# Four buffers for the experts' down weights instead of two, two of them in the memory of the transposed activations

## The chip, the cores and the metric

The kernel runs on one core of one Trainium2 chip. The metric is the device time of one execution in microseconds (us), the median of several runs.

## The reference

The kernel computes a two-layer encoder trunk for 1024 tokens of width 1024, all in float32. Layer 0 mixes tokens with a gated short convolution, layer 1 with multi-head latent attention. After each mixer stands a mixture of experts (MoE) with 64 experts; each token picks one group of eight and two experts in it. Cut to what matters here:

```
h = rms_norm(x, ffn_norm_w[i])
x = x + hier_moe(h, ...)            # once after each of the two mixers

# inside hier_moe, for every expert e of 64, over the rows sent to it:
hid = silu(xblk @ w_gate[e]) * (xblk @ w_up[e])    # 1024 -> 384
y   = hid @ w_down[e]                              # 384 -> 1024
out[token] += gate * y
```

Each of the three matrices of an expert has 1024 x 384 float32 values. There are 2 x 64 experts, 2048 assignments of a token to an expert per layer, so 32 rows for an expert on average.

## The kernel before

There are four stages one after the other: convolution, MoE of layer 0, attention, MoE of layer 1. The change is in the two MoE stages (`moe_phase`). An expert is handled in a round of at most 64 rows (`RANKS`); the loop over experts is executed 64 times in each layer here. For each expert `g`:

- GpSimd (POOL) gathers the expert's rows from `h_rows` in DRAM by an indirect DMA into `gathered` and, later, scatters the result from `y` into `y_rows`. Both use POOL's own DMA queue (q0).
- TensorE (PE) runs, in this order in its instruction stream: `gate_and_up(g)` (16 matmuls, L1230), `turn_x(g+1)` (4 transposes, L1220), `down(g-1)` (6 matmuls, L1249), `turn_h(g)` (3 transposes, L1239). So the down product of an expert stands behind the gate and up products of the next one.
- VectorE (DVE) and ScalarE (ACT) copy, multiply and apply the activation between these.
- SyncE (SP) loads the weights on one hardware DMA queue (q1): the gate matrix, the up matrix and the down matrix, 1536 KB each.

The weights have two buffers each ("slots"), expert `g` using slot `g % 2`. SP's loop walks over the experts. For expert `g` it waits until gate and up of expert `g-2` have been multiplied, issues the gate and the up load, then waits until the down product of `g-2` is done, issues the down load, and goes on to `g+1`. All counters of TensorE's products start at `AHEAD` = 2, so a wait for `g + free(0)` = `g + 1` asks for the product of expert `g - 2`. The loads of experts 0 and 1 are issued already in the stage before (`sp_store_rows`). Nothing but these waits sets when a load is issued, and SP issues them strictly in the order in which they are written.

`hT` is a tile of 128 x 8 x 1024 float32, the transposed activations, which the mixers use and which the MoE stage uses only as scratch while it works out the routing. `rows` (128 x 4 x 1024 float32) holds normalised rows before they are stored.

Of the kernel before, what the change touches and what calls it, by code (L numbers as in the profile page):

```python
# [16 lines left out]
F32 = mybir.dt.float32  # L17
I32 = mybir.dt.int32
BF16 = mybir.dt.bfloat16
# [5 lines left out]
P = 128  # L25
D, S = 1024, 1024
KD = D // P
NT = S // P
EPS = 1e-6
BANK = 512  # L30
NE, NG, EG = 64, 8, 8
NL = NG + NE
FF = 384
KF = FF // P
# [9 lines left out]
PARTS = ((HIGH, HIGH), (HIGH, LOW), (LOW, HIGH))  # L44
LATENT_AT = 12 * D
AHEAD = 2


def wait(eng, sem, value):
# [25 lines left out]
class Core:  # L75


    def __init__(self, nc, ins, out, ctx):
        self.nc, self.ins, self.out = nc, ins, out

        def sb(name, shape, dt=F32):
            return ctx.enter_context(nc.sbuf_tensor(name, shape, dt))

        self.x = sb("x", [P, NT, D])
        self.hT_at = -(-nc.sbuf_base // 32) * 32
        self.hT = sb("hT", [P, KD, S])
        self.rows = sb("rows", [P, 4, D])
        self.turned = sb("turned", [P, 2, KD, P])
        self.logits = sb("logits", [P, NT, NL])
# [299 lines left out]
class ExpertWeights:  # L389


    def __init__(self, c, layer):
        self.sems = Sems(c.nc, f"weights{layer}")
        self.gate_up_loaded = [self.sems(f"gate_up_loaded{i}") for i in range(2)]
        self.down_loaded = [self.sems(f"down_loaded{i}") for i in range(2)]
        self.piece = c.carve()
        self.gate = self.piece(2, 2, 4 * FF)
        self.up = self.piece(2, 2, 4 * FF)
        self.down = self.piece(2, KF, D)
        self.gate_dram = c.ins["exp_w_gate"][layer].rearrange("e (h p j) f -> p e h (j f)", h=2, p=P)  # L400
        self.up_dram = c.ins["exp_w_up"][layer].rearrange("e (h p j) f -> p e h (j f)", h=2, p=P)
        self.down_dram = c.ins["exp_w_down"][layer].rearrange("e (j p) d -> p e j d", p=P)
# [5 lines left out]

    def load_down(self, sp, slot, e):
        src = self.down_dram[:, bass.ds(e, 1), :, :].rearrange("p a j d -> p (a j) d")  # L410
        sp.dma_start(self.down[:, slot, :, :], src).then_inc(self.down_loaded[slot], 16)  # L411


class OutProjection:
# [449 lines left out]
def moe_phase(c, layer, last, experts):  # L864
# [4 lines left out]
    nc, ins = c.nc, c.ins  # L869
# [11 lines left out]
    idx_f = piece(4, NE)  # L881
    tiny = piece(16, NT)

    piece = c.carve(c.hT[:, :, :].rearrange("p k s -> p (k s)"))
    onehot = c.typed(f"onehot{layer}", 0, [P, 2 * NT, P], BF16, c.hT_at)
    piece(NT * P)
    by_rank = piece(2 * NT * NE)
    by_pick = piece(2, NT, EG)
# [46 lines left out]
    def free(g):  # L935
        return g + 1
# [8 lines left out]
    with nc.Block() as block:  # L945

        @block.sync
        def _(sp):
            count = rounds(sp)
            with sp.Fori(1, count * (NE // 2)) as pair:  # L950
                g = pair * 2
                for slot in range(2):
                    e = (g + slot) % NE
                    sp.wait_ge(gate_up_products, g + slot + free(0))
                    experts.load_gate_up(sp, slot, e)
                    sp.wait_ge(y_products, g + slot + free(0))
                    experts.load_down(sp, slot, e)

            sp.wait_ge(y_stored, count * NE + AHEAD)
            for t in range(NT):  # L960
                if t >= Y_RING:
                    sp.wait_ge(x_added, t - Y_RING + 1)
                src = c.y_rows.rearrange("(k t p) d -> t p k d", k=2, p=P)[t]
                sp.dma_start(y_pair[:, t % Y_RING, :, :], src).then_inc(y_pair_loaded[t % Y_RING], 16)
            if not last:
                LatentPlaces(c).load(sp, c, latents_loaded)
            if last:
                for t in range(NT):
                    sp.wait_ge(x_added, t + 1)
                    sp.dma_start(c.out[0, t * P:(t + 1) * P, :], c.x[:, t, :]).then_inc(stored, 16)  # L970
                sp.wait_ge(stored, 16 * NT)
# [230 lines left out]
        def _(pe):  # L1202
# [37 lines left out]
                                         gate_up[:, slot, j * P:(j + 1) * P], c.ident[:, :])  # L1240
                last_.then_inc(h_turned, 1)

            def down(g, slot):
                pe.wait_ge(hidden_ready, g + done(0))
                pe.wait_ge(w_down_loaded[slot], g * 8 + (16 - 8 * slot))
                pe.wait_ge(y_copied, g + free(0))
                for j in range(KF):
                    for half in range(2):
                        last_ = pe.matmul(c.ps[half * RANKS:(half + 1) * RANKS, 6 + slot, :], hidden[:, slot, j, :],  # L1249
                                          w_down[:, slot, j, half * BANK:(half + 1) * BANK],  # L1250
                                          start=(j == 0), stop=(j == KF - 1))
                last_.then_inc(y_products, 1)

            with pe.Fori(0, count) as r:
# [5 lines left out]
                last_.then_inc(idx_products, 1)  # L1260
                g0 = r * NE

                turn_x(g0, 0)
                gate_and_up(g0, 0)
                turn_x(g0 + 1, 1)
                turn_h(g0, 0)
                with pe.Fori(0, NE // 2 - 1) as pair:
                    for n in (1, 2):
                        g, slot = g0 + pair * 2 + n, n % 2
                        gate_and_up(g, slot)  # L1270
                        turn_x(g + 1, 1 - slot)
                        down(g - 1, 1 - slot)
                        turn_h(g, slot)
                gate_and_up(g0 + NE - 1, 1)
                down(g0 + NE - 2, 0)
                turn_h(g0 + NE - 1, 1)
                down(g0 + NE - 1, 1)
            if norm:
                for t in range(NT):
                    norm.pe_turn(pe, t)  # L1280
# [606 lines left out]
```

## Time and profile before

| | us |
|---|---|
| median of 3 runs | 2976.38 |
| lowest and highest run | 2976.2, 2980.21 |
| span of the profiled execution, first to last instruction | 2971.0 |
| median less span | 5.38 |

The profile shows one execution. Its span leaves out what lies around the first and the last instruction; the median of the runs stands 5.38 us above it. TensorE is busy for 81% of the span, VectorE 26%, ScalarE 22%, GpSimd 17%; the hardware queue q1 moves 666.65 MB and q0 33.64 MB. A busy share is an average over four stages with different limits, and the two MoE stages, from about 450 to 1276 us and from 2108 to 2932 us, take 1650 us of the span together.

### The profile page before, as it was taken

What the parts mean: (1) busy time and instruction counts of PE and PEld (TensorE: products, weight loads), DVE (VectorE), ACT (ScalarE), POOL (GpSimd) and SP (SyncE); (2) the same over time, 40 slices, a digit from 0 to 9 for tenths busy, and PEclk for the clock granted to TensorE, in tenths of its full rate; (3) what the DMA queues carried; (4) which work ended last, traced back from release to release, by engine and by line L of the source; (5) the groups of instructions that cost most, each with busy time, mean ns of one, the idle gap of its engine ahead of it and who ended that gap; (6) DMA issues with size and microseconds to landing.
All of it is one profiled execution on the core that took longest, in us unless ns stands there. A gap on an engine that the chain in (4) does not pass through costs nothing. (4 is left out here: it accounts for less than half of the span.)

```text
span 2971.0 us, 35580 instructions
## 1 busy us (share of the span) xinstructions
PE 2421.0 (81%) x11822; PEld 1434.1 (48%) x11822; DVE 787.3 (26%) x2377; ACT 640.3 (22%) x1328; POOL 514.2 (17%) x775
## 2 busy tenths in 40 slices
PE   7999877778878777758699999989587788787773
PEld 5888663333333333335588888768233333333331
DVE  4222650000000000050666666526200000000003
ACT  3111211111001101131255555542001111001011
POOL 2121312111111111110111111021111111111110
PEclk9999988899898988969899999999789998989897
DMA  4112037999999999950000000101799999999997
GB/s 118 43 43 85 29 156 293 390 372 390 383 388 386 395 381 390 383 187 0 8 8 9 8 15 0 57 15 73 279 381 380 395 384 383 389 383 392 382 386 298
DMA packets 202294, 701.12 MB, mean 236 GB/s; under 512 B 36192, under 2 KB 65888, under 8 KB 202224
## 3 DMA queue, kind: packets, MB, share of 16 engines
q1 hardware_dynamic: 181744, 666.65, 56.7%
q0 software_dynamic: 20480, 33.64, 3.0%
q8 instruction: 31, 0.51, 0.1%
q14 instruction: 39, 0.32, 0.0%
HBM read 687.59 MB, written 46.14 MB: 247 GB/s over the span
## 5 line engine op out<-in xcount | busy, mean ns | idle before, releaser
L1230 PE MATMUL ps<-arena 128*64 128x384 f32 x4096 | 822.4, 563 | 326.3 <-DMA arena<-in_exp_w_up 323.9
L1230 PEld LDWEIGHTS ps<-arena 128*64 128x64 f32 x4096 | 327.2, 158 | 765.6 <-issue 714.5
L1133 DVE TENSOR_TENSOR arena<-ps,xw 128x512 f32<-128x512 f32 x128 | 88.5, 691 | 1122.2 <-PE ps L1220 1122.2
L1249 PE MATMUL ps<-arena 128*64 128x512 f32 x1536 | 357.7, 600 | 2.2 <-DVE arena L1142 2.2
L1040 ACT ACTIVATE arena<-ps 128x384 f32<-128x384 f32 x128 | 62.9, 491 | 1086.2 <-PE ps L1230 1086.2
L815 PE MATMUL ps<-hT_split,w_split 128*128 128x512 f32 x1152 | 264.5, 391 | 3.1 <-DVE hT_split L291 3.1
L815 PEld LDWEIGHTS ps<-hT_split,w_split 128*128 128x128 f32 x1152 | 217.0, 189 | 49.0 <-DVE hT_split L291 3.9
L996 POOL COPY col_idx<-scatter_idx 128x1 int32 (+1 forms) x128 | 23.4, 182 | 1104.1 <-ACT arena L1051 1104.1
L1249 PEld LDWEIGHTS ps<-arena 128*64 128x64 f32 x1536 | 99.3, 136 | 164.3 <-issue 149.3
L1051 ACT ACTIVATE arena<-ps 128x512 f32<-128x512 f32 x128 | 76.4, 597 | 372.4 <-PE ps L1249 372.4
L989 POOL DMA_INDIRECT arena<-h_rows,col_idx x128 | 134.5, 1051 | 115.3 <-POOL col_idx L986 108.3
L999 POOL DMA_INDIRECT y_rows<-arena,col_idx x128 | 131.4, 1027 | 113.2 <-POOL col_idx L996 113.2
L1142 DVE TENSOR_TENSOR arena<-arena,ps 128x192 f32<-128x192 f32 x128 | 45.3, 354 | 397.4 <-ACT arena L1046 397.4
L1797 PE MATMUL ps<-arena 128*128 128x256 f32 x512 | 117.7, 384 | 7.4 <-ACT arena L1519 7.4
L1220 PEld LDWEIGHTS ps<-ident,arena 128*128 128x128 f32 x512 | 71.8, 209 | 89.0 <-issue 89.0
L1771 PE MATMUL ps<-k_split,q_split 128*128 128x512 f32 x384 | 114.7, 407 | 0.0
L1797 PEld LDWEIGHTS ps<-arena 128*128 128x128 f32 x512 | 98.1, 192 | 22.3 <-issue 8.7
L1220 PE MATMUL ps<-ident,arena 128*128 128x128 f32 x512 | 96.5, 312 | 13.2 <-DMA arena<-h_rows,col_idx 13.2
L1447 POOL TENSOR_TENSOR turned<-turned,minus_half 128x2 f32<-128x2 f32 x64 | 44.1, 689 | 355.9 <-ACT rows L1500 310.1
L1505 ACT ACTIVATE rows<-ps,turned 128x1024 f32<-128x1024 f32 x64 | 71.4, 1115 | 138.6 <-DVE turned L1675 138.6
L1672 DVE TENSOR_REDUCE turned<-ps 128x1 f32<-128x1024 f32 x64 | 78.3, 1224 | 69.4 <-PE ps L1773 67.3
L1239 PEld LDWEIGHTS ps<-ident,arena 128*128 128x128 f32 x384 | 39.8, 140 | 105.1 <-issue 102.2
(201 smaller groups left out, 2783.2 us busy)
## 6 DMA issues: line engine op xcount, KB each, us to landing
arena<-in_exp_w_gate SPq DMA_DIRECT2D x128, 1536.0 KB, 11.2
arena<-in_exp_w_up SPq DMA_DIRECT2D x128, 1536.0 KB, 14.4
arena<-in_exp_w_down SPq DMA_DIRECT2D x128, 1536.0 KB, 8.3
arena<-y_rows SPq DMA_DIRECT2D x16, 1024.0 KB, 10.9
arena<-in_conv_w_in SPq DMA_DIRECT2D x24, 512.0 KB, 3.6
h_rows<-rows SPq DMA_DIRECT2D x16, 512.0 KB, 2.6
x<-in_x SPq DMA_DIRECT2D x8, 512.0 KB, 7.5
arena<-in_conv_w_out SPq DMA_DIRECT2D x2, 2048.0 KB, 9.9
```

What stands on the lines that cost most here:

```text
L815: last = pe.matmul(c.ps[:, 3 * h + j, :], w_split[:, j, a, k, :], hT_split[:, b, k, h * BANK:(h + 1) * BANK], start=(k == 0 and a == b), s ...
L989: pool.indirect_dma_start(gathered[:, slot, :], None, h_halves, bass.IndirectOffsetOnAxis(ap=col_idx[:, slot, :], axis=0), bounds_check=2 ...
L999: pool.indirect_dma_start(y_halves, bass.IndirectOffsetOnAxis(ap=col_idx[:, 2 + slot, :], axis=0), y[:, slot, :], None, bounds_check=4 * S ...
L1051: act.activation(y[:, slot, :], c.ps[:, 6 + slot, :], ACT.Copy).then_inc(y_copied, 1)
L1133: dve.tensor_tensor(xT[:, slot, :, :, :].rearrange("p j h m -> p (j h) m"), c.ps[:, slot, :].rearrange("p (a m) -> p a m", m=RANKS), bc(c. ...
L1220: last_ = pe.transpose(c.ps[:, slot, j * P:(j + 1) * P], rows[:, j, :], c.ident[:, :])
L1230: last_ = pe.matmul(c.ps[row:row + RANKS, 2 + slot, 0:FF], xT[:, slot, j, half, :], w[:, slot, half, j * FF:(j + 1) * FF], start=(half + j ...
L1249: last_ = pe.matmul(c.ps[half * RANKS:(half + 1) * RANKS, 6 + slot, :], hidden[:, slot, j, :], w_down[:, slot, j, half * BANK:(half + 1) * ...
L1505: act.activation(probs[:, slot, :], c.ps[:, 2 * slot:2 * slot + 2, :].rearrange("p a b -> p (a b)"), ACT.Exp, bias=minus_max[:, slot, :], ...
L1672: dve.tensor_reduce(row_max[:, slot, :], c.ps[:, 2 * slot:2 * slot + 2, :].rearrange("p a b -> p (a b)"), X, ALU.max).then_inc(max_found, 1)
L1771: pe.matmul(out, q_split[:, a, 0, q], k_split[:, par, 2 * b, keys], start=(n == 0), stop=False)
L1797: last = pe.matmul(c.ps[:, 7, 0:2 * P], v[:, par, kt, :], probsT[:, j % 2, kt, :], start=(kt == 0), stop=(kt == NT - 1))
```

## The change

The down weights get four buffers (`DOWN_SLOTS` = 4), expert `g` using buffer `g % 4`. Two are the ones in the arena, the other two are placed in the memory of `hT`. The scratch of the routing, which stood in `hT`, moves into the memory of `rows`. In SP's loop the wait ahead of a down load asks for the down product of expert `g - 4` instead of `g - 2`. The order in which the loads are issued (gate, up, down of `g`, then of `g + 1`) is kept. Since the buffer numbers must be constants in the code, SP's and TensorE's loops now hold four experts in their body instead of two. TensorE's order of products is unchanged.

```
--- before.py
+++ after.py
@@ -44,6 +44,7 @@
 PARTS = ((HIGH, HIGH), (HIGH, LOW), (LOW, HIGH))
 LATENT_AT = 12 * D
 AHEAD = 2
+DOWN_SLOTS = 4
 
 
 def wait(eng, sem, value):
@@ -84,6 +85,7 @@
         self.x = sb("x", [P, NT, D])
         self.hT_at = -(-nc.sbuf_base // 32) * 32
         self.hT = sb("hT", [P, KD, S])
+        self.rows_at = -(-nc.sbuf_base // 32) * 32
         self.rows = sb("rows", [P, 4, D])
         self.turned = sb("turned", [P, 2, KD, P])
         self.logits = sb("logits", [P, NT, NL])
@@ -392,11 +394,14 @@
     def __init__(self, c, layer):
         self.sems = Sems(c.nc, f"weights{layer}")
         self.gate_up_loaded = [self.sems(f"gate_up_loaded{i}") for i in range(2)]
-        self.down_loaded = [self.sems(f"down_loaded{i}") for i in range(2)]
+        self.down_loaded = [self.sems(f"down_loaded{i}") for i in range(DOWN_SLOTS)]
         self.piece = c.carve()
         self.gate = self.piece(2, 2, 4 * FF)
         self.up = self.piece(2, 2, 4 * FF)
-        self.down = self.piece(2, KF, D)
+        down = self.piece(2, KF, D)
+        self.down = [down[:, 0, :, :], down[:, 1, :, :]]
+        for i in range(2):
+            self.down.append(c.typed(f"down{layer}_{i}", i * KF * D, [P, KF, D], F32, c.hT_at))
         self.gate_dram = c.ins["exp_w_gate"][layer].rearrange("e (h p j) f -> p e h (j f)", h=2, p=P)
         self.up_dram = c.ins["exp_w_up"][layer].rearrange("e (h p j) f -> p e h (j f)", h=2, p=P)
         self.down_dram = c.ins["exp_w_down"][layer].rearrange("e (j p) d -> p e j d", p=P)
@@ -408,7 +413,7 @@
 
     def load_down(self, sp, slot, e):
         src = self.down_dram[:, bass.ds(e, 1), :, :].rearrange("p a j d -> p (a j) d")
-        sp.dma_start(self.down[:, slot, :, :], src).then_inc(self.down_loaded[slot], 16)
+        sp.dma_start(self.down[slot], src).then_inc(self.down_loaded[slot], 16)
 
 
 class OutProjection:
@@ -881,8 +886,8 @@
     idx_f = piece(4, NE)
     tiny = piece(16, NT)
 
-    piece = c.carve(c.hT[:, :, :].rearrange("p k s -> p (k s)"))
-    onehot = c.typed(f"onehot{layer}", 0, [P, 2 * NT, P], BF16, c.hT_at)
+    piece = c.carve(c.rows[:, :, :].rearrange("p a d -> p (a d)"))
+    onehot = c.typed(f"onehot{layer}", 0, [P, 2 * NT, P], BF16, c.rows_at)
     piece(NT * P)
     by_rank = piece(2 * NT * NE)
     by_pick = piece(2, NT, EG)
@@ -947,14 +952,18 @@
         @block.sync
         def _(sp):
             count = rounds(sp)
-            with sp.Fori(1, count * (NE // 2)) as pair:
-                g = pair * 2
-                for slot in range(2):
-                    e = (g + slot) % NE
-                    sp.wait_ge(gate_up_products, g + slot + free(0))
-                    experts.load_gate_up(sp, slot, e)
-                    sp.wait_ge(y_products, g + slot + free(0))
-                    experts.load_down(sp, slot, e)
+            def refill(g, n):
+                e = (g + n) % NE
+                sp.wait_ge(gate_up_products, g + n + free(0))
+                experts.load_gate_up(sp, n % 2, e)
+                sp.wait_ge(y_products, g + n + free(0) - 2)
+                experts.load_down(sp, n % DOWN_SLOTS, e)
+
+            for n in range(2, DOWN_SLOTS):
+                refill(0, n)
+            with sp.Fori(1, count * (NE // DOWN_SLOTS)) as turn:
+                for n in range(DOWN_SLOTS):
+                    refill(turn * DOWN_SLOTS, n)
 
             sp.wait_ge(y_stored, count * NE + AHEAD)
             for t in range(NT):
@@ -1240,14 +1249,14 @@
                                          gate_up[:, slot, j * P:(j + 1) * P], c.ident[:, :])
                 last_.then_inc(h_turned, 1)
 
-            def down(g, slot):
+            def down(g, slot, w_slot):
                 pe.wait_ge(hidden_ready, g + done(0))
-                pe.wait_ge(w_down_loaded[slot], g * 8 + (16 - 8 * slot))
+                pe.wait_ge(w_down_loaded[w_slot], g * 4 + (16 - 4 * w_slot))
                 pe.wait_ge(y_copied, g + free(0))
                 for j in range(KF):
                     for half in range(2):
                         last_ = pe.matmul(c.ps[half * RANKS:(half + 1) * RANKS, 6 + slot, :], hidden[:, slot, j, :],
-                                          w_down[:, slot, j, half * BANK:(half + 1) * BANK],
+                                          w_down[w_slot][:, j, half * BANK:(half + 1) * BANK],
                                           start=(j == 0), stop=(j == KF - 1))
                 last_.then_inc(y_products, 1)
 
@@ -1260,21 +1269,25 @@
                 last_.then_inc(idx_products, 1)
                 g0 = r * NE
 
+                def expert(g, n):
+                    gate_and_up(g, n % 2)
+                    turn_x(g + 1, (n + 1) % 2)
+                    down(g - 1, (n - 1) % 2, (n - 1) % DOWN_SLOTS)
+                    turn_h(g, n % 2)
+
                 turn_x(g0, 0)
                 gate_and_up(g0, 0)
                 turn_x(g0 + 1, 1)
                 turn_h(g0, 0)
-                with pe.Fori(0, NE // 2 - 1) as pair:
-                    for n in (1, 2):
-                        g, slot = g0 + pair * 2 + n, n % 2
-                        gate_and_up(g, slot)
-                        turn_x(g + 1, 1 - slot)
-                        down(g - 1, 1 - slot)
-                        turn_h(g, slot)
+                with pe.Fori(0, NE // DOWN_SLOTS - 1) as turn:
+                    for n in range(1, DOWN_SLOTS + 1):
+                        expert(g0 + turn * DOWN_SLOTS + n, n)
+                for e in range(NE - DOWN_SLOTS + 1, NE - 1):
+                    expert(g0 + e, e)
                 gate_and_up(g0 + NE - 1, 1)
-                down(g0 + NE - 2, 0)
+                down(g0 + NE - 2, 0, DOWN_SLOTS - 2)
                 turn_h(g0 + NE - 1, 1)
-                down(g0 + NE - 1, 1)
+                down(g0 + NE - 1, 1, DOWN_SLOTS - 1)
             if norm:
                 for t in range(NT):
                     norm.pe_turn(pe, t)
```

The two places at which this shows in the instruction streams follow; semaphores are printed by the first name that their number had in the program. In SP's stream `conv_z_half` is the counter `gate_up_products` and `conv_norm_rstd_ready_0` is `y_products`. This is the whole loop body of SP in the MoE of layer 0 before, two experts:

```order
L950 ISA
L407 ISA [waits conv_z_half]
L407 DMA arena<-in_exp_w_gate 128x2x1536
L407 DMA arena<-in_exp_w_up 128x2x1536
L411 DMA arena<-in_exp_w_down 128x3x1024 [waits conv_norm_rstd_ready_0]
L954 REGISTER_ALU
L407 ISA [waits conv_z_half]
L407 DMA arena<-in_exp_w_gate 128x2x1536
L407 DMA arena<-in_exp_w_up 128x2x1536
L411 DMA arena<-in_exp_w_down 128x3x1024 [waits conv_norm_rstd_ready_0]
L950 ISA
L950 COMPARE_AND_BRANCH
```

And this is the start of the body after, the first two of four experts:

```order
L964 ISA
L412 ISA [waits conv_z_half]
L412 DMA arena<-in_exp_w_gate 128x2x1536
L412 DMA arena<-in_exp_w_up 128x2x1536
L959 REGISTER_ALU
L416 DMA arena<-in_exp_w_down 128x3x1024 [waits conv_norm_rstd_ready_0]
L957 REGISTER_ALU
L412 ISA [waits conv_z_half]
L412 DMA arena<-in_exp_w_gate 128x2x1536
L412 DMA arena<-in_exp_w_up 128x2x1536
L416 DMA arena<-in_exp_w_down 128x3x1024 [waits conv_norm_rstd_ready_0]
L957 REGISTER_ALU
```

Nothing moves past anything else: the waits and the loads stand in the same order, the register operation ahead of a down load makes the smaller value that is waited for. The third and the fourth expert of the body load into `down_0` and `down_1`, the tiles in the memory of `hT`.

On TensorE, this is one expert in the loop of the MoE of layer 0 before (`conv_g_copied` is `xT_ready`, `conv_conv_step` is `gate_up_copied`, `conv_norm_var_ready_0` is `hidden_ready`, `conv_norm_rows_ready_0` is `y_copied`, `conv_gain_loaded` and `conv_unit_used1` are `gather_done`):

```order
L1230 MATMUL ps<-arena 64x384 [waits conv_conv_step,weights0_gate_up_loaded0]
L1230 MATMUL ps<-arena 64x384 x15
L1216 ISA
L1220 MATMUL ps<-ident,arena 128x128 [waits conv_g_copied,conv_gain_loaded]
L1220 MATMUL ps<-ident,arena 128x128 x3
L1245 ISA [waits conv_norm_var_ready_0]
L1249 MATMUL ps<-arena 64x512 [waits conv_norm_rows_ready_0,weights0_down_loaded1]
L1249 MATMUL ps<-arena 64x512 x5
L1239 MATMUL ps<-ident,arena 128x128 [waits conv_norm_var_ready_0,conv_conv_step]
L1239 MATMUL ps<-ident,arena 128x128 x2
```

And one expert, the third of four in the body, after:

```order
L1239 MATMUL ps<-arena 64x384 [waits conv_conv_step,weights0_gate_up_loaded1]
L1239 MATMUL ps<-arena 64x384 x15
L1225 ISA
L1229 MATMUL ps<-ident,arena 128x128 [waits conv_g_copied,conv_unit_used1]
L1229 MATMUL ps<-ident,arena 128x128 x3
L1254 ISA [waits conv_norm_var_ready_0]
L1258 MATMUL ps<-down_0_52,arena 64x512 [waits conv_norm_rows_ready_0,weights0_down_loaded2]
L1258 MATMUL ps<-down_0_52,arena 64x512 x5
L1248 MATMUL ps<-ident,arena 128x128 [waits conv_norm_var_ready_0,conv_conv_step]
```

The sequence is the same; the six matmuls of the down product read `down_0` and wait for a semaphore of their own. Between the label of the loop and its branch back, TensorE's stream has 70 instructions in this listing before and 136 after.

## Rows read from the trace of the kernel before

**Rows 1.** The page: the span, DMA busy in 40 slices (tenths, then GB/s).

```profile
span 2971.0 us, 35580 instructions
...
DMA  4112037999999999950000000101799999999997
GB/s 118 43 43 85 29 156 293 390 372 390 383 388 386 395 381 390 383 187 0 8 8 9 8 15 0 57 15 73 279 381 380 395 384 383 389 383 392 382 386 298
```

**Rows 2.** Windows of both MoE stages: each engine's busy time, PEclk, DMA share, GB/s.

```profile
470.00:1256.00 786.00, 626.39 (x3119) 255.07 (x3117) 63.79 (x122) 79.90 (x183) 148.80 (x242) 0.90 0.96 384
2150.00:2940.00 790.00, 626.03 (x3095) 254.34 (x3091) 66.70 (x140) 80.50 (x184) 147.66 (x240) 0.90 0.94 378
```

**Rows 3.** Waits from 520 to 1240 us: us in total, times, longest.

```profile
PE ps L1230 <- DMA arena<-in_exp_w_up: 148.2, 47, 5.5
...
SPq L411 <- PE ps L1249: 623.4, 56, 14.7
```

**Rows 4.** Timeline of TensorE, one expert and the next start: start, us.

```profile
809.09 5.38 PE L1230 MATMUL ps<-arena 128*64 128x384 f32 x32
...
815.08 2.80 PE L1249 MATMUL ps<-arena 128*64 128x512 f32 x12
817.80 0.55 PE L1239 MATMUL ps<-ident,arena 128*128 128x128 f32 x3
823.19 7.07 PE L1230 MATMUL ps<-arena 128*64 128x384 f32 x32 [4.83 <-DMA arena<-in_exp_w_up]
```

**Rows 5.** Timeline of SP's queue at the same place: issues of loads.

```profile
808.72 0.37 SPq L411 DMA_DIRECT2D arena<-in_exp_w_down  x1
809.38 0.37 SPq L407 DMA_DIRECT2D arena<-in_exp_w_gate  x1
...
817.91 0.37 SPq L411 DMA_DIRECT2D arena<-in_exp_w_down  x1
```

**Rows 6.** Windows, columns as in Rows 2: a gap, then two stretches of 20 us.

```profile
809.00:810.00 1.00, 1.00 (x8) 0.48 (x8) 0.34 (x1) 0.62 (x2) 0.18 (x1) 1.00 0.61 61
810.00:811.00 1.00, 1.00 (x8) 0.43 (x6) 0.01 (x1) 0.00 (x0) 0.28 (x1) 1.00 0.49 201
811.00:812.00 1.00, 1.00 (x8) 0.43 (x6) 0.00 (x0) 0.00 (x0) 0.94 (x2) 1.00 0.96 319
...
813.00:833.00 20.00, 15.16 (x75) 6.27 (x73) 1.74 (x3) 1.80 (x4) 3.31 (x5) 0.91 1.02 422
...
1226.00:1246.00 20.00, 14.77 (x73) 5.93 (x69) 1.74 (x3) 1.80 (x4) 2.46 (x4) 0.83 1.00 413
```

**Rows 7.** Timelines: each layer's first load in the loop, and its last gate/up product.

```profile
460.83 0.40 SPq L407 DMA_DIRECT2D arena<-in_exp_w_gate  x1
...
1261.07 8.29 PE L1230 MATMUL ps<-arena 128*64 128x384 f32 x32 [3.81 <-DMA arena<-in_exp_w_up]
...
2117.31 0.39 SPq L407 DMA_DIRECT2D arena<-in_exp_w_gate  x1
...
2916.79 8.16 PE L1230 MATMUL ps<-arena 128*64 128x384 f32 x32 [3.63 <-DMA arena<-in_exp_w_up]
```

**Rows 8.** DMA queues and issues, 520 to 1240 us: packets, MB, share; median to landing.

```profile
q1 hardware_dynamic: 52726, 263.43, 90.8%
q0 software_dynamic: 8936, 14.80, 5.4%
...
arena<-in_exp_w_down SPq DMA_DIRECT2D x56, 1536.0 KB, 8.3
```

**Rows 9.** The page: instruction loads of the whole execution.

```profile
q8 instruction: 31, 0.51, 0.1%
```

**Rows 10.** Timeline of TensorE: two gate/up products behind a short idle time.

```profile
950.76 8.14 PE L1230 MATMUL ps<-arena 128*64 128x384 f32 x32 [3.23 <-DMA arena<-in_exp_w_up]
...
2747.53 5.38 PE L1230 MATMUL ps<-arena 128*64 128x384 f32 x32 [1.62 <-DMA arena<-in_exp_w_up]
```

**Rows 11.** The page: transposes of the gathered rows, idle time and its releaser.

```profile
L1220 PE MATMUL ps<-ident,arena 128*128 128x128 f32 x512 | 96.5, 312 | 13.2 <-DMA arena<-h_rows,col_idx 13.2
```

## The prediction

> **What bounds the kernel now.** I read the page's slices first. Where the two MoE stages stand, the DMA digits are 9 nearly throughout at 372 to 395 GB/s [rows 1]; elsewhere DMA is mostly idle. The windows over each stage give 384 and 378 GB/s at a DMA share of 0.96 and 0.94, while TensorE is busy 626 us of 786 and of 790 [rows 2]. So the weights' stream sets the pace of both stages, and TensorE waits for it. The waits say the same: TensorE sat 148.2 us of 720 idle in front of gate/up products until an up load landed [rows 3]. The question is whether the stream runs as fast as it can. A share of 0.96 looks full, so I opened the stream in steps of 1 us. In 813 to 833 us it moves 422 GB/s; just before, in the three microseconds from 809, it moves 61, 201 and 319 [rows 6]. The stream is not limited throughout, it has gaps, and a packet that waits at the start of a flow counts as busy, which is why the share hides them.
>
> **Where a gap comes from.** SP's queue waited 623.4 us, in 56 of 56 experts, for the down product (L1249) ahead of the down load [rows 3]. The two timelines side by side show it. The down load is issued at 808.72, when a down product has ended, and the gate load behind it only at 809.38, although the gate/up product that frees that buffer had ended before that down product began; a gate/up product then starts at 809.09, so all that had been loaded was being used up, and the stream was empty [rows 4, 5]. The next expert's issue (817.91) falls into a running stream. So there is about one gap for two experts. The expert that waits, at 823.19, had TensorE idle for 4.83 us [rows 4].
>
> **The change, part by part.** Expert g's down load now waits for the down product of g-4, which is always long done when gate and up of g-2 have ended. So it goes out right behind the gate and up loads of the same expert, and SP stands at the next wait for gate/up. When TensorE starts gate/up of g-1 (its up load has just landed), SP has already issued down g-1, gate and up g, and down g: four loads of 1.573 MB (1536 KB), 6.3 MB, which take 14.9 us at 422 GB/s. TensorE's product ends 5.38 to 8.29 us later [rows 4, 7], and gate and up of g+1 are queued behind at least 6.6 us of work. The stream should never run empty again; the order of loads is the same, so no load lands later than it does now relative to the bytes ahead of it.
>
> Now the sum. From the first load in the loop to the start of the last gate/up product layer 0 takes 1261.07 - 460.83 = 800.2 us, layer 1 2916.79 - 2117.31 = 799.5 us [rows 7]. In it 62 gate, 62 up and 61 down loads are moved: 185 x 1.573 = 291.0 MB. POOL's queue moves 14.80 MB in 56 experts, 0.264 for one [rows 8], so 16.4 MB for 62. Together 307.4 MB; 307.4 / 800.2 us is 384 GB/s, as the window says. Unbroken, the rate is that of the stretch without a gap, 422, or of the slower one, 413 [rows 6]. I take 420, nearer to the first since gap-free stretches like it are the more common: 731.9 us. The stream must start once: after an issue at 808.72 the rate is short by 0.3 us and by 361, 221 and 103 KB in the three windows, 1.9 us together [rows 6]. That makes 733.8 us, a gain of 66.4 and 65.7 us, 132 us for both. Against the profiled span 2971.0 that is 2839, and against the median of the runs, which stands 5.4 us above the span, 2976.4 - 132.1 = 2844.3.
>
> What costs nothing, and what covers it:
> - The register operations and the longer loop body of SP: SP waited 623.4 us of 720, 11 us for each expert [rows 3]. If this cover were gone a load would be issued some tenths late, into a stream that still has 6.6 us of work.
> - TensorE's work for one expert is 818.35 - 809.09 = 9.26 us [rows 4], against 733.8 / 62 = 11.84 us of stream. What TensorE waits for is then each gate/up load, about 2.6 us, instead of every second for 3 to 5.
> - Gather and scatter: TensorE waited for a gather 13.2 us in all [rows 11], at the starts. A gather is issued two experts ahead, and stays so with 11.8 us for an expert instead of 12.9.
> - The scratch in another tile: same instructions, same sizes.
> - The down load of the last expert lands some 3.7 us after its up load; its gate/up product takes 5.38 us or more. The chain behind it is unchanged.
>
> **The clock.** After 3.23 us of idle time TensorE's gate/up product took 8.14 us, after 1.62 us 5.38 us [rows 10]; the granted clock there is 0.5 (1.2 GHz) for the first microseconds and 1.0 (2.4 GHz) otherwise. An idle time of 2.6 us lies between. If every product took 8.14 us, an expert would take 9.26 + 2.76 = 12.02 us, more than 11.84; but then TensorE has no idle time before the next product, which speaks against the low clock there. I count nothing, for the loss as for the gain at the two last products (2 x 2.8 us, if they find the full clock).
>
> **A rule on the ceiling.** The trace's gap-free stretch has 422 GB/s [rows 6]. The Trainium skill, DMA: Bandwidth & Descriptors, section Where 436 GB/s comes from, derives 435 GB/s from 16 ports; an estimate by it is 307.4 / 435 = 706.7 us for a layer, 25 us less than mine. The same section says that from HBM some 358 GB/s bind, by which there would be nothing to gain; the trace's average of 384 is already above that, and the measurement decides.
>
> **The rivals.**
> - The stream runs unbroken but slower than the short stretches. Its packets took 90.8 + 5.4% of 720 us for 56 experts [rows 8], 12.37 us each. If that is what an expert costs, 62 take 767 us, plus 1.9: a gain of 31 us per layer, 2976 - 62 = 2914. Against it: the share is 1.02 in a gap-free stretch and the packets in the gap are counted long. With 413 GB/s it is 744.3 + 1.9 = 746.2 us, a gain of 107: 2869. Chance of 2870 to 2915: 0.13.
> - TensorE becomes the bound through its clock: 12.02 us for each of 62 experts, 745 us and 1.9, a gain of 53 per layer: 2870; worse if transposes and down products are slowed too, to about 2890. Chance 0.05.
> - The change doesn't do what it says: SP's queue takes no further load while some are under way, or the gap has another releaser. Then 2976. Against it: SP issued the down load at 817.91 while the pair of 809.38 was under way [rows 5]. Chance 0.03.
> - Slower: TensorE's loop body is twice as long, 136 listed instructions, and its code is loaded anew on each turn. It decides if a turn of four experts stalls for more than the 4 x 2.6 = 10.4 us of idle time that it hides in and the 132 us / 30 turns = 4.4 us gained, 14.8 us; at 20 us it gives 2976 + 30 x 5.2 = 3132. Against it: 31 instruction packets in the whole execution [rows 9], of which none falls into 520 to 1240 us, and attention's loop of TensorE, 541 listed instructions, loads none by that queue either between 1670 and 1920 us. Chance 0.02.
> The Trainium skill, Runtime: NRT & Kernel Launch, section Instruction fetch mechanics, says that a taken branch whose target is outside the current window of two pages forces a fetch before execution goes on; it would make this rival likelier. By that rule, the trace would show loads in attention's loop, and shows none on that queue.
>
> **How the numbers follow.** The forecast, 2844, has chance 0.77; its own range is 2828 (423 GB/s, 2 us more, and the last products at full clock, 5.6, and some noise of the start) to 2869 (413 GB/s). The range for 8 in 10 takes that and the near end of the first two rivals: 2827 to 2874. A run can be told from no change by about 0.2%, 6 us. Faster by more: 0.77 + 0.13 + 0.05 less 0.01 for the unforeseen = 0.94; within: 0.03; slower: 0.03.
>
> **What the profile after would show.** Windows over the MoE stages at about 420 GB/s and no 1 us window under 380 inside; SP's long wait at the gate/up load instead of the down load; gate/up products at a regular distance of 11.8 us, each behind 2 to 3 us of idle time until an up load lands; 733 us from first load to last gate/up product. The prediction is wrong if the rate without gaps falls below 410, if gaps remain, or if TensorE has no idle time left.

## The result, and the profile after

The changed kernel takes 2858.06 us (median of 4 runs, 2857.32 to 2859.57) against 2976.29 us, a ratio of 0.9622 with a 95% interval of 0.9595 to 0.9648. (The 2976.29 us is the median of four runs of the kernel before, of which one took 2961.33.) The forecast was 2844, the range 2827 to 2874. The profiled execution has a span of 2857.8 us, 113.2 less than the one before.

From the page of the kernel after: the span, the DMA rows of the 40 slices, the instruction queue, and the loads with their median time to landing in us.

```profile
span 2857.8 us, 35460 instructions
...
DMA  4111127999999999850000000100599999999997
GB/s 116 52 44 60 51 105 294 423 421 421 415 414 407 414 412 413 356 184 0 8 9 9 9 8 8 59 8 38 219 423 422 422 421 416 412 415 408 405 406 285
...
q8 instruction: 35, 0.57, 0.1%
...
arena<-in_exp_w_down SPq DMA_DIRECT2D x64, 1536.0 KB, 20.6
down<-in_exp_w_down SPq DMA_DIRECT2D x64, 1536.0 KB, 20.7
```

The slices that read 372 to 395 GB/s before [rows 1] begin at 423 now. They don't stay there: in both MoE stages they slide to 405 to 416 in the second half. A down load takes 20.6 us to land where it took 8.3 [rows 8], because it is now issued early and stands in the queue; that is not a cost.

The waits of the kernel after, 520 to 1160 us (us in total, times, longest), TensorE's first, then SP's queue:

```profile
PE ps L1239 <- DMA arena<-in_exp_w_up: 104.9, 52, 3.3
```

```profile
SPq L412 <- PE ps L1239: 539.0, 53, 13.0
```

SP's wait for the down product is gone. It waits in front of the gate load (L412) for the buffer of gate and up. TensorE waits for a load at 52 experts of 53, but never for more than 3.3 us, where it waited up to 5.5 [rows 3]. Timelines of the kernel after, one expert on TensorE (start, us), then SP's issues:

```profile
519.18 7.05 PE L1239 MATMUL ps<-arena 128*64 128x384 f32 x32 [2.36 <-DMA arena<-in_exp_w_up]
526.15 0.75 PE L1229 MATMUL ps<-ident,arena 128*128 128x128 f32 x4
526.84 2.79 PE L1258 MATMUL ps<-arena 128*64 128x512 f32 x12
529.56 0.55 PE L1248 MATMUL ps<-ident,arena 128*128 128x128 f32 x3
531.25 5.38 PE L1239 MATMUL ps<-arena 128*64 128x384 f32 x32 [1.15 <-DMA arena<-in_exp_w_up]
```

```profile
526.45 0.37 SPq L412 DMA_DIRECT2D arena<-in_exp_w_gate  x1
526.91 0.42 SPq L412 DMA_DIRECT2D arena<-in_exp_w_up  x1
527.51 0.37 SPq L416 DMA_DIRECT2D arena<-in_exp_w_down  x1
```

The three loads of an expert leave together when the gate/up product ends. The down load no longer waits for the four microseconds of transposes and down product that follow [rows 5]. And the ends of the stage, which answer to [rows 7], from the timelines of SP's queue and TensorE:

```profile
460.32 0.38 SPq L412 DMA_DIRECT2D arena<-in_exp_w_gate  x1
...
1205.96 5.38 PE L1239 MATMUL ps<-arena 128*64 128x384 f32 x32 [2.42 <-DMA arena<-in_exp_w_up]
...
2058.69 0.37 SPq L412 DMA_DIRECT2D arena<-in_exp_w_gate  x1
...
2805.24 7.08 PE L1239 MATMUL ps<-arena 128*64 128x384 f32 x32 [2.59 <-DMA arena<-in_exp_w_up]
```

Layer 0 takes 745.6 us from the first load to the last gate/up product, layer 1 746.6, where 733.8 were forecast and 800.2 and 799.5 measured before. The gain is 54.6 + 52.9 us of 113.2. The last products, at a higher clock, give 2.9 and 1.1 more; the rest of 1.7 us is spread.

So the main mechanism held, and some 12 us for each layer are missing. Windows of 100 us in the stage of layer 0 (busy time of each engine, then PEclk, DMA share, GB/s) show where:

```profile
470.00:570.00 100.00, 83.75 (x429) 34.29 (x427) 8.72 (x17) 11.29 (x26) 22.19 (x36) 0.93 1.02 423
570.00:670.00 100.00, 85.50 (x440) 34.96 (x440) 8.68 (x17) 10.97 (x25) 19.74 (x32) 0.93 1.02 421
670.00:770.00 100.00, 83.63 (x423) 33.93 (x419) 9.09 (x18) 11.30 (x26) 20.33 (x34) 0.93 1.02 417
770.00:870.00 100.00, 83.54 (x418) 34.16 (x420) 8.37 (x16) 10.48 (x24) 21.61 (x35) 0.92 1.02 416
870.00:970.00 100.00, 84.97 (x438) 34.92 (x434) 8.37 (x16) 10.75 (x25) 19.74 (x32) 0.93 1.01 407
```

Averaged over 100 us, the DMA share stays at 1.02 or 1.01 while the bytes fall from 423 to 407 GB/s. In the list of the trace's packets, those of 6144 bytes (gate and up) take 234 ns as a rule. From 770 to 1140 us 483 of 15781 took over 250 ns, some over 1000; before the change it was 55 of 14759.

An average over 100 us hides where this happens, as it did before the change. Here are SP's gate loads and TensorE around 1010 us, then steps of 1 us:

```profile
994.83 0.37 SPq L412 DMA_DIRECT2D arena<-in_exp_w_gate  x1
...
1009.81 0.37 SPq L412 DMA_DIRECT2D arena<-in_exp_w_gate  x1
```

```profile
1001.23 8.36 PE L1239 MATMUL ps<-arena 128*64 128x384 f32 x32 [2.72 <-DMA arena<-in_exp_w_up]
```

```profile
1008.00:1009.00 1.00, 1.00 (x8) 0.42 (x6) 0.00 (x0) 0.00 (x0) 0.00 (x0) 1.00 1.02 422
1009.00:1010.00 1.00, 1.00 (x8) 0.48 (x4) 0.00 (x0) 0.36 (x1) 0.00 (x0) 1.00 0.69 283
1010.00:1011.00 1.00, 1.00 (x7) 0.42 (x7) 0.61 (x1) 0.13 (x1) 0.00 (x0) 1.00 0.67 156
1011.00:1012.00 1.00, 1.00 (x8) 0.32 (x6) 0.08 (x1) 0.00 (x0) 0.00 (x0) 1.00 0.66 207
```

The gate/up product began at 1001.23 and took 8.36 us, at the lower level of the clock for a good part (1.2 GHz, a granted clock of 0.50, in the microsecond from 1006). Only then did SP issue the next loads, 15 us after the last ones. Meanwhile the share fell to 0.69 and the rate to 283, 156 and 207 GB/s: some of the DMA engines had nothing left to move. The packets say how many. Eleven begin between 1010.85 and 1011.09 us and take 0.68 to 1.3 us, where 0.23 is usual, about a microsecond behind the issue, just as ten packets do behind the issue at 460.32 us, which finds the stream empty (they begin from 461.42 to 461.68 us and take 0.74 to 0.96 us). At a share near 1 the 16 engines have about one packet each under way, so some eleven of the 16 had run empty. The stream has gaps again, partial and rare ones.

These gaps carry most of what is missing. I added up the packets' bytes, each spread evenly over its packet's time, and compared them with 422 GB/s. From 770 to 1195 us 10.0 us' worth of bytes is missing, 8.2 of it in the four microseconds behind the 35 issues of a gate load. Of these 8.2, 7.7 stand behind the 18 issues whose gate/up product took 6.7 to 8.4 us, and 0.5 behind the 17 whose product took the 5.38 us of the full clock. In layer 1, from 2400 to 2790 us, it is 11.7 in all, 9.7 behind the issues, and 9.2 of that behind the slow products. From 470 to 770 us it is only 1.3, though 11 of 25 products were slow there too. So it takes two things at once: a late issue, and engines that have come apart.

How far the engines are apart shows where the stage's last load ends. These are the first and the last microsecond of that end in layer 0 of the change, and the only one of the kernel before:

```profile
1204.00:1205.00 1.00, 0.00 (x0) 0.00 (x0) 0.35 (x1) 0.00 (x0) 0.12 (x2) 1.00 0.37 143
...
1209.00:1210.00 1.00, 1.00 (x10) 0.46 (x8) 0.00 (x0) 0.00 (x0) 0.00 (x0) 1.00 0.06 25
```

```profile
1264.00:1265.00 1.00, 1.00 (x6) 0.28 (x4) 0.00 (x0) 0.00 (x0) 0.00 (x0) 0.50 0.43 170
```

Before the change the stream goes from 412 GB/s to nothing within about a microsecond: all engines end together. After it they end one by one over six microseconds (1204 to 1210): they have drifted apart. The prediction counted on at least 6.6 us of work behind every issue. That is the work of an engine in the middle of the field; for one that is six microseconds ahead hardly any is left.

### The profile page after: what moved, and what is told of

It is laid out like the page before. It is cut to its first block and busy times, and to the rows that moved or that the text cites. A ratio compares the mean times of both kernels' runs of the same rounds, so it can differ in the third digit from the quotient of the medians.

```text
span 2857.8 us, 35460 instructions
## 1 busy us (share of the span) xinstructions
PE 2391.4 (84%) x11822; PEld 1423.9 (50%) x11822; DVE 787.4 (28%) x2377; ACT 640.2 (22%) x1328; POOL 515.3 (18%) x775
## 5 line engine op out<-in xcount | busy, mean ns | idle before, releaser
L1239 PE MATMUL ps<-arena 128*64 128x384 f32 x4096 | 792.8, 546 | 243.5 <-DMA arena<-in_exp_w_up 241.4
L1239 PEld LDWEIGHTS ps<-arena 128*64 128x64 f32 x4096 | 317.1, 153 | 663.8 <-issue 460.3
L1258 PE MATMUL ps<-down,arena 128*64 128x512 f32 x768 | 178.8, 600 | 2.2 <-DVE arena L1151 2.2
L1258 PE MATMUL ps<-arena 128*64 128x512 f32 x768 | 178.9, 601 | 0.0
L1008 POOL DMA_INDIRECT y_rows<-arena,col_idx x128 | 131.8, 1030 | 113.2 <-POOL col_idx L1005 113.2
## 6 DMA issues: line engine op xcount, KB each, us to landing
arena<-in_exp_w_down SPq DMA_DIRECT2D x64, 1536.0 KB, 20.6
```

What stands on the lines that cost most here:

```text
L1008: pool.indirect_dma_start(y_halves, bass.IndirectOffsetOnAxis(ap=col_idx[:, 2 + slot, :], axis=0), y[:, slot, :], None, bounds_check=4 * S ...
L1239: last_ = pe.matmul(c.ps[row:row + RANKS, 2 + slot, 0:FF], xT[:, slot, j, half, :], w[:, slot, half, j * FF:(j + 1) * FF], start=(half + j ...
```

## The experiments

The kernels ran in two groups of four, each group on one chip, where the kernel before took 2961.13 and 2965.42 us; so the ratios are compared, and not the times. The changed kernel itself stands in the second group.

**The wait alone.** Four buffers, their places, the moved scratch and the long loops stay; the wait is the old one.

```
-                sp.wait_ge(y_products, g + n + free(0) - 2)
+                sp.wait_ge(y_products, g + n + free(0))
```

> The changed kernel with four down buffers, but the down load of expert g waits for the down product of g-2 again, as before. Theory A (the gain is the wait alone: the down load no longer holds back the queue, so the stream has no gaps): the gaps come back, 384 GB/s over a MoE stage, 2976 us within 0.3%. Rival B (the buffers' place in memory, or the loop bodies of four experts, or the moved scratch give part of the gain): below 2965 us.

Measured: 2965.68 us beside 2961.13, ratio 1.0015 (1.0003 to 1.0027). The window over 700 us of the stage of layer 0 (columns as above):

```profile
470.00:1170.00 700.00, 560.55 (x2767) 227.38 (x2765) 56.82 (x109) 71.49 (x164) 133.04 (x218) 0.90 0.95 384
```

384 GB/s is the rate of before [rows 2]. The whole gain is the wait. The longer loops, the place in `hT` and the scratch in `rows` give nothing and cost about 0.15%, 0.27% at the far end of the interval.

**A shorter queue.** The down load of g waits for the down product of g-3: one character, `- 1` in place of `- 2` in the same line.

> The changed kernel, the down load of g waits for the down product of g-3, so three buffers would do. The load is issued about 4 us later than in the change, into a stream that still has the gate and up load of its expert to move. Theory A (only an empty stream costs): same as the change, 2858 us within 0.2%. Rival C (the 12 us per layer that the change missed are engines of the DMA that ran out of work because too little was queued): less queued, so slower than the change, 2865 us or more.

Measured: 2863.76 us (2855.41 to 2865.57), ratio 0.9661 (0.9645 to 0.9678). The changed kernel in the second group has 0.9642 (0.9627 to 0.9656), so the intervals overlap and the two can't be told apart; beside 0.9622 of the first result it would be slower by 0.4%. So the time does not decide between theory A and rival C. The trace of the change above shows that rival C is right about the cause: engines did run out of queued work. This run takes nothing from the point at which it hurts, though, since gate and up are issued as before. Long packets are somewhat more, 659 of 15725. With three buffers' worth of waiting the gain is still 3.4%, nearly all of it.

**No row traffic.** Gather and scatter move only row 0; the experts' part of the output is left out.

```
-                                        bounds_check=2 * S - 1, oob_is_err=False).then_inc(gather_done[slot], 16)
+                                        bounds_check=0, oob_is_err=False).then_inc(gather_done[slot], 16)
...
-                                        bounds_check=4 * S - 1, oob_is_err=False).then_inc(scatter_done[slot], 16)
+                                        bounds_check=0, oob_is_err=False).then_inc(scatter_done[slot], 16)
...
-                src = c.y_rows.rearrange("(k t p) d -> t p k d", k=2, p=P)[t]
-                sp.dma_start(y_pair[:, t % Y_RING, :, :], src).then_inc(y_pair_loaded[t % Y_RING], 16)
+                src = c.h_rows.rearrange("(t p) d -> t p d", p=P)[t]
+                for k in range(2):
+                    sp.dma_start(y_pair[:, t % Y_RING, k, :], src).then_inc(y_pair_loaded[t % Y_RING], 16)
```

> The changed kernel without the bytes of gather and scatter: both move only row 0 (their bound is 0), and the rows added at the end of a stage are read from h_rows; its output leaves the experts out. 291.0 MB remain for a layer. Theory D (POOL's row packets, unevenly spread over the 16 DMA engines, are what drives the engines apart and slows their packets in the later half of a stage): no packets over 250 ns for 6144 bytes, 425 GB/s flat through the stage, 685 us from first load to last gate/up product, 2736 us. Theory E (the long unbroken stream slows by itself, whatever POOL moves): the slices still fall from about 425 to 410 GB/s late in each stage, 705 us, about 2775 us.

Measured: 2752.57 us (one run). Windows late in the stage, and the last gate/up product of layer 0, whose first load was issued at 459.78:

```profile
870.00:970.00 100.00, 86.08 (x457) 35.53 (x453) 8.87 (x18) 11.78 (x27) 22.12 (x36) 0.97 1.02 421
970.00:1070.00 100.00, 87.61 (x456) 35.76 (x455) 9.41 (x18) 11.29 (x26) 22.12 (x36) 0.95 1.02 421
```

```profile
1154.42 5.38 PE L1240 MATMUL ps<-arena 128*64 128x384 f32 x32 [1.95 <-DMA arena<-in_exp_w_up]
```

The decline is gone, and so are the long packets (0 of 16924 from 770 to 1140 us). At its end the stream falls from 369 GB/s to nothing in about two microseconds (1156 to 1158), not in six. Theory D's rate of 425 was too high, the flat rate is 421 to 422: 291.0 / 422 + 1.9 = 691.5 us against 694.6 measured. Theory E, that a long stream slows by itself, falls. So does the thought that small packets do it: the change has 3142 packets of 8 bytes on POOL's queue from 500 to 1100 us, this run 6818.

**Stops.** At every 16th expert the down load waits until gate and up of its own expert have landed, which lets the stream run empty.

```
-            def refill(g, n):
+            def refill(g, n, meet=False):
...
-                sp.wait_ge(y_products, g + n + free(0) - 2)
+                if meet:
+                    sp.wait_ge(landed, g + n + done(0))
+                else:
+                    sp.wait_ge(y_products, g + n + free(0) - 2)
...
+            with sp.Fori(1, count * (NE // 16)) as turn:
+                for n in range(16):
+                    refill(turn * 16, n, n == 0)
...
                 pe.wait_ge(w_gate_up_loaded[slot], g * 16 + (32 - 16 * slot))
+                pe.sem_inc(landed, 1)
```

> The changed kernel; at every 16th expert the down load waits until gate and up of the same expert have landed (TensorE counts this), so the stream runs empty on purpose 3 times per layer and all 16 DMA engines start level again. Theory F (the engines drift apart in an unbroken stream and then get in each other's way): rate back to 421 GB/s behind each stop and no long decline, 728 + 2 + 3 x 2 = 736 us for a layer instead of 745.6, so about 2839 us. Rival G (the slower rate late in a stage has to do with the place in the weights or with time, not with drift): the decline stays and the stops add 3 x 2 us for each layer, 2870 us.

Measured: 2867.5 us (2862.83 to 2868.53), ratio 0.9677 (0.9664 to 0.969); the first load of layer 0 is at 461.35 and its last gate/up product at 1210.58, 749.2 us. One stop in steps of 1 us, and the long stretch behind it:

```profile
634.00:635.00 1.00, 1.00 (x10) 0.55 (x8) 0.00 (x0) 0.00 (x0) 0.00 (x0) 1.00 1.02 420
635.00:636.00 1.00, 1.00 (x8) 0.30 (x4) 0.00 (x0) 0.00 (x0) 0.00 (x0) 1.00 0.78 320
636.00:637.00 1.00, 1.00 (x8) 0.75 (x8) 0.16 (x1) 0.49 (x1) 0.00 (x0) 1.00 0.47 197
637.00:638.00 1.00, 1.00 (x6) 0.29 (x4) 0.53 (x1) 0.00 (x0) 0.00 (x0) 1.00 0.35 147
638.00:639.00 1.00, 1.00 (x8) 0.29 (x4) 0.00 (x0) 0.00 (x0) 0.00 (x0) 1.00 0.29 123
639.00:640.00 1.00, 1.00 (x7) 0.31 (x3) 0.00 (x0) 0.35 (x1) 0.00 (x0) 1.00 0.19 80
640.00:641.00 1.00, 0.01 (x1) 0.00 (x0) 0.35 (x1) 0.47 (x2) 0.18 (x1) 1.00 0.04 18
641.00:642.00 1.00, 0.89 (x6) 0.57 (x8) 0.00 (x0) 0.00 (x0) 0.44 (x1) 1.00 0.00 0
```

```profile
650.00:780.00 130.00, 107.14 (x545) 47.60 (x544) 10.81 (x21) 13.84 (x32) 27.04 (x44) 0.92 1.02 423
```

This is the row that shows the drift. The last bytes of one load are due, and the DMA share falls from 1.02 over 0.47, 0.29 and 0.19 to nothing: the 16 DMA engines have drifted apart and end one after the other over nearly six microseconds. Without that they end together (before the change, at 1264 us), so the late ones had been held up on the way. Behind the stop the rate is 423 for 130 us, where the change had slipped to 421 and 417, and the long packets drop from 483 to 33. Half of theory F is right: the engines drift, and level engines bring the rate back. Its time is wrong, because a stop must wait for the last engine; that the result is near rival G's 2870 is chance, since the decline that G wants is gone. With 730.3 us for an unbroken 422 GB/s, three stops cost 18.9 us, 6.3 each and not 2.

**More stops.** The same with 8 for 16.

> The kernel of the stops, with a stop at every 8th expert instead of every 16th, 7 for each layer. The stop at 16 took about 7 us of the stream, with the engines finishing one by one over some 6 us, not the 2 us of an empty start. Theory F2 (the spread grows with the bytes since the last level start): a stop costs about 1.9 + half of the rest, 4.5 us, so 31 us for a layer against 20 with three stops: 2865 + 2 x 11 = 2887 us. Rival I (the cost of a stop is fixed, about 7 us): 7 x 7 = 49 us for a layer, 2865 + 2 x 28 = 2921 us.

Measured: 2888.19 us (2885.17 to 2892.49), ratio 0.9734 (0.9717 to 0.9752). Layer 0 takes 1223.25 - 461.73 = 761.5 us, so seven stops cost 31.2 us, 4.5 each, as F2 had it. So the spread grows with the bytes moved since the engines were level, from 8 experts to 16. It doesn't go on in proportion: after all 62 experts of the change it is again about six microseconds, eight in the profile of the changed kernel run again (1202 to 1210). That is what one would expect if an engine far ahead must wait for the next issue; it is argued, and no run shows it. No packet of 15360 is long.

**Half the row traffic.** Only the gather's bound is set to 0 (the first of the edits under "No row traffic"); the experts' part of the output is left out.

> The changed kernel with the gather moving only row 0, the scatter left whole; the output leaves the experts out. POOL's bytes are halved: 291.0 + 62 x 0.132 = 299.2 MB. If the decline comes from unevenness in gather and scatter alike, it is about half as deep as in the change, an average of 417 to 420 GB/s, 715 us for a layer, 2797 us. If the scatter's writes to DRAM alone made it, 413 GB/s, 726 us, 2819 us. If the gather alone made it, flat 422, 711 us, 2789 us.

Measured: 2796.57 us (one run), against 2797 expected if gather and scatter have an equal part. Layer 0 takes 1174.45 - 457.34 = 717.1 us. The third and the sixth window of its stage:

```profile
670.00:770.00 100.00, 85.12 (x443) 34.78 (x441) 9.41 (x18) 11.79 (x27) 21.07 (x35) 0.95 1.02 422
...
970.00:1070.00 100.00, 84.49 (x437) 34.60 (x433) 9.41 (x18) 11.79 (x27) 20.26 (x34) 0.95 1.02 418
```

The decline comes later and is shallower, with 160 long packets of 16405. The time alone, one run, would not exclude that the gather made it all (2789); the 418 GB/s and the long packets do, since the scatter alone brings them about.

**Even row traffic, and twice as much.** Places without a token get the index of row 0 instead of one out of bounds, so every gather and scatter moves 128 half rows. The output is wrong for token 0.

```
-                in_round.mark(dve.tensor_scalar(idx_f[:, 2, :], code, 0.5, 1e6, ALU.is_lt, ALU.mult))
+                in_round.mark(dve.tensor_scalar(idx_f[:, 2, :], code, 0.5, 2.0, ALU.is_lt, ALU.mult))
```

> The changed kernel with gather and scatter always moving all 128 half rows of 2 KB: a place without a token reads and writes row 0, so the output is wrong for token 0. POOL's bytes double to 0.524 MB for an expert, and are the same for each of the 16 DMA engines. Theory D2 (it is the unevenness of POOL's packets over the engines that drives them apart): no decline, 422 GB/s through the stage though more is moved; 291.0 + 62 x 0.524 = 323.5 MB, 766.6 + 1.9 us for a layer, 2858 + 2 x 23 = 2904 us. Rival H (POOL's traffic as such slows the weights' packets, even or not): the decline is deeper than in the change, below 410 GB/s on average, 2945 us or more. Many writes to one row may disturb, which would speak for H wrongly.

Measured: 2902.81 us (one run), layer 0 in 1226.99 - 460.12 = 766.9 us. The page's slices and POOL's queue, then the window over the stage:

```profile
GB/s 116 49 44 86 23 144 296 423 424 423 423 423 424 423 423 423 409 184 0 8 9 9 8 16 0 58 8 44 261 423 424 424 424 421 424 424 424 424 424 315
...
q0 software_dynamic: 20480, 67.13, 5.7%
```

```profile
470.00:1170.00 700.00, 574.25 (x2894) 233.79 (x2891) 58.97 (x113) 74.16 (x170) 140.09 (x228) 0.92 1.02 423
```

This tells D2 and H apart most sharply. POOL moves twice the bytes and the stream does not decline at all: 423 GB/s to the end, 19 long packets of 15350. The gate/up products are slow as often as in the change, 16 of 34 from 770 to 1195 us, up to 8.37 us, and nothing is missing behind their issues; the last load ends within about two microseconds (1229 to 1231). So a late issue does no harm while the engines are level. That the rows' shares of the engines are what this run evens out is inferred from the indices, because the trace doesn't name a packet's engine. Traffic beside the weights is harmless here when all places of gather and scatter are filled. It costs its own bytes, no more: 766.9 us, with 766.6 + 1.9 expected.

**The change again.**

> The changed kernel once more, unaltered, beside the others of this call on one chip, since the kernel before ran about 0.5% faster in the first call of experiments than beside the prediction's result. Expected ratio to before 0.9622 again, within 0.003, and the wait for g-3 and the three stops therefore slower than it by 0.4 and 0.6%. If the ratio is 0.966 or more here, the wait for g-3 is the same as the change.

Measured: 2858.89 us (2858.28 to 2861.02) beside 2965.42, ratio 0.9642 (0.9627 to 0.9656). The changed kernel takes the same time in both measurements, 2858.06 and 2858.89 us; it is the kernel before that differs, by 0.4%. The intervals of the two ratios overlap. The three stops are slower than this by 0.4%; the wait for g-3 can't be told from it. Its trace repeats the account above: 9.4 us' worth of bytes is missing from 770 to 1195 us, 7.0 behind the issues and 6.5 of that behind slow products.

## Why the prediction was right, and where it was off

- The reading of the bound was right. The stages ran at 384 and 378 GB/s with a share of 0.96 and 0.94, and there was something to win in a stream that looked busy.
- The cause of the gap was right, and the experiment with the old wait shows that it is all of it: ratio 1.0015 with everything else of the change in place.
- The step that did not hold is "The stream should never run empty again". Its cover, at least 6.6 us of work behind every issue (9.5 with a product of 5.38 us), is worked out for all engines together. Late in a stage they are six to eight microseconds apart, and those ahead run out: 156 GB/s at 1010 us, at a share of 0.67.
- In the sum this is the rate of the unbroken stream. I took 420 GB/s and 731.9 us from stretches of 20 us. Over a stage it is 307.4 MB / (745.6 - 1.9) us = 413 GB/s. The text had 413 as the far end of its range, read from a window that ran slower, so that the result falls into the range says little about the reason. Before the change a gap about every two experts let the engines come level again, so no gap-free window of that trace could show the decline. The two layers lack 11.8 and 12.8 us, 24.6 together; the last products and the rest give 5.7 back, which leaves the 18.9 us between the forecast gain of 132.1 and the 113.2 of the spans. The medians lie 118.2 apart, since that of after stands 0.3 us above its span and that of before 5.3 above its own; in the second group the gain is only 106.5 us (2965.42 less 2858.89).
- The first rival's numbers are near this (2869 for 413 GB/s), though not its reason. It blamed the packets' busy time at all places alike; what happened is that engines waited behind late issues in the second half of a stage.
- The clock was counted at nothing, and that is wrong by the traces. The idle time of 2.6 us was seen, 1.2 to 3.3. Behind it the gate/up product takes 5.38 us at about half of the experts and 6.7 to 8.4 at the others, so both levels of the clock occur. TensorE itself catches up, because it waits again before the next product. But SP issues the next gate load only when the product has ended, so a slow product delays the issue by up to 3 us, and 7.7 of the 8.2 us missing behind issues in layer 0 stand behind such products. No run changes the clock alone.
- The slower rival did not happen. The instruction queue q8 has 35 packets in place of 31 [rows 9] for the longer code, and none of them falls into 520 to 1140 us or 2160 to 2780 us. The Trainium skill, Runtime: NRT & Kernel Launch, section Instruction fetch mechanics, has a taken branch out of a window of two pages force a fetch. By that rule, no trace here shows a loop of this size to be outside of it.
- Of the signs named ahead, "no 1 us window under 380" was wrong (156 GB/s at 1010 us, 133 at 2778), and the distance of two gate/up products is 12.0 us on average and uneven, 11.5 to 12.9.

What is shown, then: uneven row traffic drives the engines apart (the runs without rows and with even rows, and the ends of the streams), level engines bring the rate back (the stops), and the bytes that are missing are missing mostly behind late issues. A packet that waits while its engine has no work counts as busy and looks long, which explains part of the long packets. Others are only 300 to 450 ns long and stand five to nine microseconds behind an issue, as at 1100 us; whether these are engines that read different parts of DRAM at one time, no run here tells. Also untested is the remedy that this points to, a third buffer for gate and up, with which SP could issue earlier. The stops and the even rows repair the rate and lose the gain by their own cost, so no version tried beats the changed kernel.

## What to carry to other kernels

When a queue is in order and one load in it waits for a later event than the loads behind it, give that load more buffers before anything else: here one wait moved was 3.6 to 3.8% of the time. A DMA share of 0.96 is no proof of a full stream; look at it in steps of a microsecond, and price the gaps by the rate beside them. A rate read between gaps holds only for stretches of that length, since gaps also put parallel DMA engines level: here a long stream with uneven traffic beside it ran 2% slower. And when you work out how much queued work covers a late issue, leave room for the engine that is furthest ahead, and take the slowest product, not the usual one.

## What the runs showed of the hardware

- The 16 DMA engines are not kept in step by a stream of large loads. From the first load of the stage to the first of the stops, at 641 us, they spread by nearly 6 us. In the unbroken stream of the change the last load of the stage ends over six microseconds, before the change within about one. The Trainium skill, DMA: Bandwidth & Descriptors, section Queues, rings and completion order, has a DMA split over up to 16 rings, one for each engine, each with a tail pointer of its own. The trace agrees in so far as the parts of one load end at different times.
- A queue that looks four loads deep can be empty for some engines: at 1010 us the share was 0.67 and the rate 156 GB/s, while the average over 100 us had a share of 1.02 or 1.01.
- Even traffic of two queues shares the engines without loss: 423 GB/s with 0.524 MB of rows for each expert.
- The highest sustained rate from DRAM into the core's memory was 421 to 424 GB/s here, 423 over 700 us with even rows.
